# Half sums of two passes joined by accumulating transfers, rotation of quarter columns, and index scores in PSUM, in a hybrid decode step

## The chip, the cores and the metric

One core of one Trainium2 chip. The metric is device time in microseconds of one execution of the whole program. The engines named are TensorE (PE; its weight loads PEld), VectorE (DVE), ScalarE (ACT), GpSimd (POOL) and SyncE (SP, which only issues transfers here).

## What is computed

One layer of a hybrid decoder step over 1024 prompt tokens and 64 sample tokens (together TOK = 1088) with a model width of 2048. In float32 throughout:

```python
h = rmsnorm(x, g) * (1 + scale) + shift            # scale, shift, gate from silu(c) @ w_ada + b_ada
q_a,k_a,v_a,z_a,q_b,k_b,v_b,z_b,q_i,k_i,w_i,g_a,g_b = split(h @ w_in)
# q_a, k_a, q_b, k_b and the indexer's q_i, k_i are rotated by position
# branch A: dilated windows (128,1), (512,4), (2048,16), merged by their softmax denominators
# branch B: I[t,s] = sum_h w_i[t,h] * relu(q_i[t,h] . k_i[s]); top 256 keys of each query, attention over those
y = x + gate * ((sigmoid(g_a) * ((o_a*silu(z_a)) @ w_pa) + sigmoid(g_b) * ((o_b*silu(z_b)) @ w_pb)) @ w_out)
y = rmsnorm(y, g_final)                            # keys and values are outputs too
```

`h @ w_in` is the largest part: 76 column tiles of 128 besides the three of the indexer.

## The kernel before, in words

Everything lies transposed: a column of the projection is a tile of 128 partitions by 1088 tokens. Each factor of a product is split into a high and a low part (`h_hi`, `h_lo`, `wc_hi`, `wc_lo`), and three matmuls make one full product.

**Start (to about 150 us).** Rows are normed, transposed and modulated; the adaLN weights are streamed; products for the first two indexer tiles run among them. SP saves the upper half of `h` into the scratch `merged`.

**Index (about 150 to 264 us).** `third_products` makes the third indexer tile. `leave_index` rotates the tiles out of PSUM into `qi_t` and `ki_two` through `rot_a` and `rot_b`. Then for each of seven query tiles (`PICKS`, widths 384 to 1088) and four heads PE makes scores, ACT writes their relu into `relu_s` (SBUF, two buffers), and DVE multiplies by `wi_tok` and sums into `acc` (`index_scores`), which SP stores in the scratch `score`. POOL meanwhile makes the activation sums S1 to S4 of the scheme below, once `ki_two` is stored.

**Two passes of steps.** The projection is done by pairs of columns with a seven-product scheme over quarters (two halves of tokens, FIRST and SECOND, and even and odd tiles of the inner dimension). The inner dimension is halved too: steps 0 to 37 (`PAIRS` = 38) make all column pairs over the first half, steps 38 to 75 over the second. A step is products P1, P4 of the step before, P2, P6, P5, P7, P3. Their results leave the banks as quarters "11", "12", "22", "21" of a `col` tile (two buffers): copies by ACT (`act_out_of`) and additions by DVE (`add_bank`). P6, P7 and P3, P4 accumulate onto banks that must have been read out before (`p1_out`, `u2_out`, `p5_out`, `c22_out`, `c21_out`). Each engine's order is written out by hand in `pe`'s `step`, `act_step`, `dve_step`, `pool_step`, `sp_step`. The weights of the next step are summed on POOL (`weight_sums`, line 2548 is the first of its four), and split by ACT (`high_weights`), DVE (`low_weights_dve`) and POOL (`low_weights`).

In the first pass SP stores each half sum in the scratch `proj`. In the second SP loads it back into `col` ahead of the step (`load_part`). DVE adds "11", "12", "22" to it from the bank (`direct`), or ACT copies the bank into `snap` and POOL adds that (`add_snap`). The second pass takes first the rotated columns: 2 + 4 (kind "class") + 2 + 4 + 1 pairs, then 3 plain pairs, then 22 whose columns get SiLU or sigmoid ("curved", `act_ended`). Rotation is done in the step: DVE multiplies the swapped halves by sine (`swapped`), POOL the column by cosine (`by_cosine`), DVE adds (`turned`); class columns go out regrouped through `turn_o`.

**Picks.** The top 256 of each query tile are found by 32 rounds on DVE (`pick_round`, lines 2301 and 2303: the eight largest, then strike them out of `work`), spread over the steps through `rounds`. SP loads `work` and stores the mask. Picks 0 to 3 lie in steps 2 to 36 with four rounds a step and one step without rounds between picks, picks 4 to 6 in steps 53 to 73 with four or five and none between.

**After the passes (from about 2060 us)** come attention of both branches and the merge with the output projection.

## Time and profile before

| | us |
|---|---|
| median of three runs | 3195.18 (3194.44 to 3195.89) |
| the profiled execution | 3194.12 |
| its span, first to last instruction | 3192.6 |
| busy in it: PE, DVE, POOL, ACT | 2918.5, 2176.8, 1171.8, 1030.2 |

A profile is one execution. "Busy" is time in which an engine worked on an instruction; the granted clock is TensorE's, 1.00 being 2.4 GHz. A wait names who ended it. Line numbers are those of the kernel before.

### The profile page before, as it was taken

What the parts mean: (1) busy time and instruction counts of PE and PEld (TensorE: products, weight loads), DVE (VectorE), ACT (ScalarE), POOL (GpSimd) and SP (SyncE); (2) the same over time, 40 slices, a digit from 0 to 9 for tenths busy, and PEclk for the clock granted to TensorE, in tenths of its full rate; (3) what the DMA queues carried; (4) which work ended last, traced back from release to release, by engine and by line L of the source; (5) the groups of instructions that cost most, each with busy time, mean ns of one, the idle gap of its engine ahead of it and who ended that gap; (6) DMA issues with size and microseconds to landing.
All of it is one profiled execution on the core that took longest, in us unless ns stands there. A gap on an engine that the chain in (4) does not pass through costs nothing. (4 is left out here: it accounts for less than half of the span.)

```text
span 3192.6 us, 56880 instructions
## 1 busy us (share of the span) xinstructions
PE 2918.5 (91%) x21635; PEld 2728.3 (85%) x21635; DVE 2176.8 (68%) x2948; ACT 1030.2 (32%) x1748; POOL 1171.8 (37%) x1096
## 2 busy tenths in 40 slices
PE   5858999999999888889988988989999999999998
PEld 4736999999999888889987888978877897998987
DVE  4496876877767698997887878556654553654655
ACT  5214333223232321112332323266433332333333
POOL 3162666643333365565554545433224101000000
PEclk8979999999999999999999999999999999999999
DMA  9923455444454543434443434466259775584673
GB/s 348 366 65 105 143 165 178 157 156 150 134 162 128 202 139 119 133 133 149 143 134 126 138 130 134 154 216 192 87 157 293 236 249 182 179 274 130 206 238 99
DMA packets 415737, 544.88 MB, mean 171 GB/s; under 512 B 29572, under 2 KB 327236, under 8 KB 412484
## 3 DMA queue, kind: packets, MB, share of 16 engines
q1 hardware_dynamic: 401478, 498.50, 49.1%
q0 software_dynamic: 12944, 42.23, 4.1%
q8 instruction: 83, 1.36, 0.2%
q10 hardware_dynamic: 1152, 2.13, 0.2%
q14 instruction: 80, 0.66, 0.1%
HBM read 407.84 MB, written 137.04 MB: 171 GB/s over the span
## 5 line engine op out<-in xcount | busy, mean ns | idle before, releaser
L3118 PE MATMUL banks<-h_hi,wc_lo 128*128 128x272 f32 x4256 | 1242.0, 292 | 0.0
L3116 PE MATMUL banks<-h_hi 128*128 128x272 f32 x2432 | 720.3, 296 | 107.5 <-DVE col L2880 58.4
L3118 PEld LDWEIGHTS banks<-h_hi,wc_lo 128*128 128x128 f32 x4256 | 816.2, 192 | 0.0
L3117 PE MATMUL banks<-h_lo,h_hi 128*128 128x272 f32 x2432 | 714.8, 294 | 0.0
L3116 PEld LDWEIGHTS banks<-h_hi 128*128 128x128 f32 x2432 | 471.8, 194 | 119.5 <-issue 57.4
L3116 PE MATMUL banks<-h_hi,wc_hi 128*128 128x272 f32 x1824 | 530.4, 291 | 23.4 <-ACT col L2700 15.2
L3117 PE MATMUL banks<-h_lo,wc_hi 128*128 128x272 f32 x1824 | 528.1, 290 | 0.0
L3117 PEld LDWEIGHTS banks<-h_lo,h_hi 128*128 128x128 f32 x2432 | 472.5, 194 | 0.0
L3116 PEld LDWEIGHTS banks<-h_hi,wc_hi 128*128 128x128 f32 x1824 | 345.5, 189 | 29.8 <-issue 29.0
L3117 PEld LDWEIGHTS banks<-h_lo,wc_hi 128*128 128x128 f32 x1824 | 345.8, 190 | 0.0
L2029 DVE TENSOR_TENSOR u_lo<-u_raw,u_hi 128x1536 fp32r<-128x1536 f32 (+1 forms) x96 | 195.8, 2039 | 202.8 <-ACT u_hi L1943 202.4
L2880 DVE TENSOR_TENSOR col<-banks,col 128x544 f32<-128x544 f32 x309 | 220.8, 720 | 135.4 <-PE banks L3118 126.2
L2301 DVE MAX8 best<-work 128x8 f32<-128x1088 f32 x224 | 287.7, 1284 | 19.3 <-DMA work<-scratch_score 17.9
L1943 ACT CAST u_hi<-u_raw 128x1536 fp32r<-128x1536 f32 (+1 forms) x96 | 162.8, 1696 | 414.0 <-PE banks L2287 232.0
L2680 ACT CAST h_hi<-xn_t 128x512 fp32r<-128x512 f32 x304 | 188.8, 622 | 305.5 <-PE banks L3118 183.9
L2303 DVE MATCH_REPLACE8 work<-best,work 128x1088 f32<-128x1088 f32 x224 | 285.9, 1276 | 0.6 <-issue 0.6
L2854 DVE TENSOR_TENSOR wc_lo<-raw,wc_hi 128x512 fp32r<-128x512 f32 x152 | 158.0, 1040 | 164.0 <-ACT wc_hi L2680 163.6
L2680 ACT CAST wc_hi<-raw 128x512 fp32r<-128x512 f32 x228 | 141.2, 620 | 343.0 <-PE banks L3118 343.0
L2854 DVE TENSOR_TENSOR wc_lo<-xn_t,h_hi 128x512 fp32r<-128x512 f32 x228 | 225.6, 990 | 32.7 <-ACT h_hi L2680 24.1
L2576 POOL TENSOR_TENSOR wc_lo<-raw,wc_hi 128x512 fp32r<-128x512 f32 x76 | 101.0, 1329 | 360.7 <-ACT wc_hi L2680 360.5
L2285 PE MATMUL banks<-u_hi,m_hi 128*128 128x512 f32 x512 | 200.5, 392 | 5.6 <-DVE u_lo L2029 5.6
L2287 PE MATMUL banks<-u_lo,m_hi 128*128 128x512 f32 x512 | 200.2, 391 | 0.0
(340 smaller groups left out, 5374.8 us busy)
## 6 DMA issues: line engine op xcount, KB each, us to landing
scratch_proj<-col SPq DMA_DIRECT2D x144, 544.0 KB, 4.1
raw<-in_w_in SPq DMA_DIRECT2D x76, 1024.0 KB, 5.9
u_raw<-in_w_out SPq DMA_DIRECT2D x96, 512.0 KB, 5.0
col<-scratch_proj SPq DMA_DIRECT2D x76, 544.0 KB, 3.6
ada_w<-in_w_ada SPq DMA_DIRECT2D x16, 2048.0 KB, 14.0
u_raw<-in_w_pb SPq DMA_DIRECT2D x48, 512.0 KB, 4.9
gate_w<-in_w_ada SPq DMA_DIRECT2D x16, 1024.0 KB, 5.9
u_raw<-in_w_pa SPq DMA_DIRECT2D x48, 256.0 KB, 3.2
```

Of the source, the lines that this page charges most:

```text
L1943: nc.scalar.copy(u_hi[u % 2][:, 0:ks, :], u_raw[:, u, 0:ks, :]).then_inc(u_hi_set, 1)
L2029: nc.vector.tensor_tensor(u_lo[u % 2][:, 0:ks, :], u_raw[:, u, 0:ks, :], u_hi[u % 2][:, 0:ks, :], ALU.subtract).then_inc(u_lo_set, 1)
L2285: nc.tensor.matmul(dst, high, hi[:, x, :], start=first, stop=False)
L2287: mm = nc.tensor.matmul(dst, high, lo[:, x, :], start=False, stop=last)
L2301: nc.vector.max(best8[:], work[:])
L2303: nc.vector.match_replace(work[:], best8[:], work[:], TAKEN)
L2680: nc.scalar.copy(wc_hi(c), src).then_inc(wc_hi_set, 1)
L2854: nc.vector.tensor_tensor(wc_lo[c][:], src, wc_hi(c), ALU.subtract).then_inc(lo_dve, 1)
L2880: nc.vector.tensor_tensor(dst, pair_bank(bank), dst, ALU.add).then_inc(out, 1)
L3116: nc.tensor.matmul(dst, hi[:, j, :], high, start=(fresh and j == 0), stop=False, skip_group_check=True)
L3117: nc.tensor.matmul(dst, hi[:, j, :], low, start=False, stop=False, skip_group_check=True)
L3118: mm = nc.tensor.matmul(dst, lo[:, j, :], high, start=False, stop=(j == KB - 1), skip_group_check=True)
```

## The change

Four parts.

1. **Second pass.** A second-pass step now leaves its banks as a first-pass step does. Then `add_halves`, on POOL's queue, joins the two halves of the inner dimension by a transfer that accumulates: into `proj` in DRAM (`proj += col`) for rotated and plain columns, into `col` (`col += proj`) for curved ones, on which ACT then works and which SP stores. `load_part`, `snap` and `add_snap` go.
2. **Rotation.** Rotated columns are read back by quarters of tokens, 104 blocks, four in each of the steps 40 to 52 and 54 to 66: SP loads the quarter, and once more with its halves swapped (`load_rotated`), DVE makes two products and a sum (`rotate`), SP stores. Block b+1 is loaded behind the store of block b. The tables hold half of the tokens at a time. Class columns go into the scratch `merged`.
3. **Index.** Relu writes back into PSUM, and DVE reads PSUM; PE's banks are free after DVE's sum (`acc_step`) instead of after the relu. The third indexer weights and the tables are loaded ahead of the stores of `h`. POOL's sums come before the store of `ki_two`, in two pieces each; the first block is split ahead of the last query tile.
4. **Picks.** Picks 0 to 4 lie in steps 2 to 36, five and four rounds a step, with no step between; picks 5 and 6 in steps 39 to 54 and 56 to 71 with two rounds a step.

The core of the diff:

```diff
-        for x in range(4):
-            for s in range(2 + 9 * x, 10 + 9 * x):
-                PICK_ROUNDS[s] = (x, 4)
-        PICK_LATE = SNAP_STEPS[0] + 1
-        for x in range(3):
+        for x in range(5):
             for y in range(7):
-                PICK_ROUNDS[PICK_LATE + 7 * x + y] = (4 + x, 5 - y % 2)
+                PICK_ROUNDS[2 + 7 * x + y] = (x, 5 - y % 2)
+        for x in range(2):
+            for y in range(16):
+                PICK_ROUNDS[PAIRS + 1 + 17 * x + y] = (5 + x, 2)
...
+        ROT_COLS = [(s, q) for s in TURN_STEPS for q in range(2)]
+        ROT_BLOCKS = [(s, q, 2 * half + y) for half in range(2) for s, q in ROT_COLS for y in range(2)]
+        HALF_BLOCKS = len(ROT_BLOCKS) // 2
+        ROT_AT = {b: PAIRS + 2 + b // 4 + b // HALF_BLOCKS for b in range(len(ROT_BLOCKS))}
...
                     if h == 0:
-                        nc.vector.tensor_scalar(out, relu_s[:, n % 2, 0:width], wi_tok[:, t, h:h + 1], None,
+                        nc.vector.tensor_scalar(out, flat(pick_bank(n), P, width), wi_tok[:, t, h:h + 1], None,
                                                 ALU.mult).then_inc(acc_step, 1)
...
+        def load_rotated(sp, b):
+            (s, q, y), g = ROT_BLOCKS[b], b % 2
+            ts, lo, up = slice(y * PC, (y + 1) * PC), slice(0, HD // 2), slice(HD // 2, HD)
+            src = scr["proj"][T0_OF(s) + q]
+            sp.wait_ge(added[s % 2][q], 16 * added_cols(s))
+            if b >= 2:
+                sp.wait_ge(rot_out[g], rot_outs(b - 2))
+            sp.dma_start(rot_x[:, g, 0, :], src[:, ts]).then_inc(rot_in[g], 16)
+            for to, of in ((lo, up), (up, lo)):
+                sp.dma_start(rot_x[to, g, 1, :], src[of, ts]).then_inc(rot_in[g], 16)
...
+        def rotated_at(sp, s, j):
+            if (s, j) in ROT_IN:
+                b = ROT_IN[s, j]
+                store_rotated(sp, b)
+                if b == HALF_BLOCKS - 1:
+                    load_tables(sp, 1)
+                if b + 1 < len(ROT_BLOCKS):
+                    load_rotated(sp, b + 1)
...
+        def add_halves(pool, s, q):
+            par = s % 2
+            if s == PAIRS:
+                for x in range(2):
+                    pool.wait_ge(col_stored[x][q], 16 * stored_cols(PAIRS, x))
+            for out in ((c11_out, c21_out), (c22_out, c12_out))[q]:
+                pool.wait_ge(out, s + 1)
+            ours, half = col[par][:, q, :], scr["proj"][T0_OF(s) + q]
+            if curved(s):
+                pool.dma_start(ours, half, accum_op=ALU.add).then_inc(added[par][q], 16)
+            else:
+                pool.dma_start(half, ours, accum_op=ALU.add).then_inc(added[par][q], 16)
...
         def pool_step(pool, s):
             low_weights(pool, s, 5)
-            if s and turns(s - 1):
-                by_cosine(pool, s - 1, 2)
-            if snaps(s):
-                add_snap(pool, s, 0)
+            if s > PAIRS:
+                add_halves(pool, s - 1, 1)
             low_weights(pool, s, 6)
-            if s and turns(s - 1):
-                by_cosine(pool, s - 1, 3)
+            if s > PAIRS:
+                add_halves(pool, s - 1, 0)
             if s + 1 < STEPS:
                 weight_sums(pool, s + 1)
...
-                    nc.scalar.activation(relu_s[:, n % 2, 0:width], flat(pick_bank(n), P, width),
+                    nc.scalar.activation(flat(pick_bank(n), P, width), flat(pick_bank(n), P, width),
                                          ACT.Relu, scale=IH ** -0.5 * ID ** -0.5).then_inc(relu_set, 1)
...
+        def rotate(dve, b):
+            (s, _, y), g = ROT_BLOCKS[b], b % 2
+            ts, x, swapped = slice(y % 2 * PC, (y % 2 + 1) * PC), rot_x[:, g, 0, :], rot_x[:, g, 1, :]
+            dve.wait_ge(rot_in[g], 48 * (b // 2 + 1))
+            dve.wait_ge(rot_ready, 80 + 48 * (b // HALF_BLOCKS))
+            nc.vector.tensor_tensor(x, x, rot_cos[:, ts], ALU.mult).then_inc(rot_mul, 1)
+            nc.vector.tensor_tensor(swapped, swapped, rot_sin[:, ts], ALU.mult).then_inc(rot_mul, 1)
+            dve.wait_ge(rot_mul, 2 * b + 2)
+            if not by_class_of(b):
+                nc.vector.tensor_tensor(x, x, swapped, ALU.add).then_inc(rot_add, 1)
+                return
...
         def rounds(dve, s, n):
+            if (s, n) in ROT_IN:
+                rotate(dve, ROT_IN[s, n])
...
-            parts = ((0, 1, 2, 2) if late else (1, 1, 1, 1)) if all_ == 4 else ((0, 1, 2, 2) if late else (1, 1, 1, 2))
+            parts = (0, 1, 0) if all_ == 2 else (0, 1, 2) if late else (1, 1, 1)
```

## Rows read from the trace of the kernel before

**Rows 1.** Windows by stage: busy time and instructions of each engine, PEclk, DMA, GB/s.
```profile
150.00:264.00 114.00, 62.73 (x372) 36.92 (x370) 99.05 (x98) 29.42 (x46) 50.65 (x14) 0.76 0.30 94
264.00:1083.00 819.00, 812.62 (x6814) 807.91 (x6807) 599.51 (x720) 253.09 (x435) 393.12 (x312) 1.00 0.47 149
1083.00:2060.00 977.00, 852.49 (x6404) 838.42 (x6404) 784.37 (x848) 254.61 (x389) 509.21 (x351) 0.95 0.42 138
```

**Rows 2.** Timeline of POOL: start, duration; the first weight sum of a step.
```profile
343.12 1.30 POOL L2548 TENSOR_TENSOR xn_t<-raw 128x512 f32<-128x512 f32 x1 [0.17 <-POOL wc_lo L2576]
...
364.23 1.29 POOL L2548 TENSOR_TENSOR xn_t<-raw 128x512 f32<-128x512 f32 x1 [0.17 <-POOL wc_lo L2576]
...
1083.18 1.30 POOL L2548 TENSOR_TENSOR xn_t<-raw 128x512 f32<-128x512 f32 x1 [0.17 <-POOL wc_lo L2576]
...
1123.46 1.55 POOL L2548 TENSOR_TENSOR xn_t<-raw 128x512 f32<-128x512 f32 x1 [0.17 <-POOL wc_lo L2576]
...
1151.72 1.29 POOL L2548 TENSOR_TENSOR xn_t<-raw 128x512 f32<-128x512 f32 x1
...
1672.96 1.29 POOL L2548 TENSOR_TENSOR xn_t<-raw 128x512 f32<-128x512 f32 x1 [0.17 <-POOL wc_lo L2576]
...
1707.28 1.29 POOL L2548 TENSOR_TENSOR xn_t<-raw 128x512 f32<-128x512 f32 x1 [0.17 <-POOL wc_lo L2576]
...
2037.65 1.29 POOL L2548 TENSOR_TENSOR xn_t<-raw 128x512 f32<-128x512 f32 x1 [0.17 <-POOL wc_lo L2576]
```

**Rows 3.** Waits from 1083 to 2060 us: who, for whom, total, times, longest.
```profile
ACT col L2714 <- DVE col L2880: 242.4, 38, 17.1
POOL col L2571 <- ACT snap L2708: 198.2, 27, 18.4
```

**Rows 4.** DVE instructions on tile col: count, shortest, median, longest in ns.
```profile
L2880 DVE TENSOR_TENSOR col<-banks,col x203: 707/718/728, 1050.1 to 2073.3; 128x544 f32<-128x544 f32 x102
...
L2905 DVE TENSOR_TENSOR col<-col,turn_b x36: 712/1795/1802, 1131.3 to 1460.9; 128x544 f32<-128x544 f32 x36
```

**Rows 5.** DMA issues: count, KB each, median us from issue to landing.
```profile
col<-scratch_proj SPq DMA_DIRECT2D x76, 544.0 KB, 3.6
...
gates<-scratch_proj SPq DMA_DIRECT2D x64, 192.0 KB, 2.4
...
scratch_resid<-prep_lo POOLq DMA_DIRECT2D x8, 544.0 KB, 4.7
```

**Rows 6.** Timeline of SP where it issues transfers back to back: start, duration.
```profile
2070.26 0.38 SPq L737 DMA_DIRECT2D k_t<-scratch_proj  x1
2070.68 0.51 SPq L737 DMA_DIRECT2D v_t<-scratch_proj  x1
```

**Rows 7.** Timeline of DVE in two first-pass steps and at one change of pick.
```profile
598.24 1.28 DVE L2301 MAX8 best<-work 128x8 f32<-128x1088 f32 x1
...
601.02 1.50 DVE L2854 TENSOR_TENSOR wc_lo<-xn_t,h_hi 128x512 fp32r<-128x512 f32 x1
...
613.07 1.29 DVE L2854 TENSOR_TENSOR wc_lo<-raw,wc_hi 128x512 fp32r<-128x512 f32 x1 [2.01 <-ACT wc_hi L2680]
...
617.94 0.73 DVE L2880 TENSOR_TENSOR col<-banks,col 128x544 f32<-128x544 f32 x1 [0.95 <-PE banks L3118]
...
1683.76 1.29 DVE L2301 MAX8 best<-work 128x8 f32<-128x1088 f32 x1 [8.96 <-DMA work<-scratch_score]
```

**Rows 8.** Timeline of DVE in the index stage; in brackets its idle time before.
```profile
156.75 1.29 DVE L364 TENSOR_TENSOR w_lo<-w_raw,w_hi 128x1088 fp32r<-128x1088 f32 x1 [12.91 <-DMA irot_sin<-in_rot]
...
191.39 7.75 DVE L2344 TENSOR_SCALAR acc<-relu_s,wi_tok 128x384 f32<-128x384 f32 x1 [0.60 <-ACT relu_s L2841]
...
199.27 14.99 DVE L2347 SCALAR_TENSOR_TENSOR acc<-relu_s,wi_tok,acc 128x384 f32<-128x384 f32 x3
```

**Rows 9.** Timeline of PE: the third products, and P1 of the first step.
```profile
158.09 0.59 PE L392 MATMUL banks<-h_hi,w_hi 128*68 128x384 f32 x1 [7.50 <-DVE w_lo L364]
...
264.05 0.39 PE L3116 MATMUL banks<-h_hi,wc_hi 128*128 128x272 f32 x1
```

More of the change, by code:

```diff
@@ L456, in decode_step @@
         turns = lambda s: kind_of(s) in ("turned", "class")
-        direct = lambda s: turns(s) or s > 0 and turns(s - 1)
-        snaps = lambda s: s >= PAIRS and not direct(s)
         curved = lambda s: s >= PAIRS and not isinstance(kind_of(s), str)
@@ L2336, in index_scores @@
                     low_weights_dve(dve, 0, 1)
+                    low_block(dve, 0)
                 if width < TOK:
@@ L2865, in add_bank @@
         def add_bank(dve, s, x, bank, place, out):
-            q = int(x[1]) - 1
             dve.wait_ge(p_done, done(s, place))
-            if s >= PAIRS:
-                dve.wait_ge(part_landed[s % 2][q], 16 * sum(y % 2 == s % 2 for y in range(PAIRS, s + 1)))
-            if x != "21" and out not in (p1_out, u2_out, p5_out):
-                n = ("11", "12", "22").index(x)
-                if snaps(s):
-                    dve.wait_ge(snap_added, 3 * before(s, snaps) + n + 1)
-                else:
-                    dve.wait_ge((p1_out, u2_out, p5_out)[n], s + 1)
@@ L2877, in add_bank @@
[L2877 to L2878 removed]
+            copied = {"11": p1_out, "12": u2_out, "22": p5_out, "21": e_out}[x]
+            dve.wait_ge(copied, 1 if x == "21" else s + 1)
             dst = of_col(s % 2, x)
             nc.vector.tensor_tensor(dst, pair_bank(bank), dst, ALU.add).then_inc(out, 1)
[L2882 to L2895 removed]
@@ L2931, in dve_step @@
         def dve_step(dve, s):
-            par, more, rot = s % 2, s + 1 < STEPS, turns(s)
-            was = s and turns(s - 1)
+            par, more = s % 2, s + 1 < STEPS
             if s:
@@ L2937, in dve_step @@
                 low_block(dve, 7)
-            if was:
-                turned(dve, s - 1, 1)
-                swapped(dve, s - 1, 2)
-            if direct(s):
-                add_bank(dve, s, "11", BANK_A(par), "P1", p1_out)
             if more:
@@ L2945, in dve_step @@
             rounds(dve, s, 0)
-            if was:
-                turned(dve, s - 1, 2)
-            if s > PAIRS:
-                add_bank(dve, s - 1, "21", BANK_A(1 - par), "P4", c21_out)
-            if was:
-                swapped(dve, s - 1, 3)
             if s == PAIRS:
@@ L2954, in dve_step @@
             add_bank(dve, s, "11", BANK_B, "P2", c11_out)
-            if was:
-                turned(dve, s - 1, 3)
-            if rot:
-                swapped(dve, s, 0)
             if more:
@@ L3140, in step @@
             need(pe, x_lo_set, x_waits[1])
-            need(pe, relu_set, scores)
+            need(pe, acc_step, scores)
             need(pe, c11_out, s)
@@ L3296, in _ @@
                 for h0 in range(0, IH, 2):
-                    need(pe, relu_set, n - 2)
+                    need(pe, acc_step, n - 2)
                     for a in range(0, width, 512):
@@ L3308, in _ @@
             for h in range(IH):
-                need(pe, relu_set, n - (h > 0))
+                need(pe, acc_step, n - (h > 0))
                 half = slice(ID * (h % 2), ID * (h % 2) + ID)
@@ L3320, in _ @@
                 n += 1
-            pe.wait_ge(relu_set, n - 1)
+            pe.wait_ge(acc_step, n - 1)
             step(pe, 0, 0, x_waits=(0, 0, 1, 2, 3, 4, 0), scores=n)
```

344 lines of the change are left out of this document (144 added, 200 removed).

## The prediction

> **What bounds the kernel now.** I read the windows by stage first, then the clock of the steps, then the waits inside the slow stretch, then single instructions.
>
> [Rows 1] cut the span into stages. Up to 150 us the transfers set the pace and the change hardly touches it; after 2060 us comes attention and merging, which it touches only at the seam. From 264 to 1083 us (first pass of the 38 column pairs) TensorE is busy 812.6 of 819 us at full clock: nothing to win there, only to lose. Two stretches are not PE-bound. From 150 to 264 us (index scores) PE is busy 62.7 of 114 us, the granted clock is 0.76 and DVE is busy 99 us. From 1083 to 2060 us (second pass, the same products) PE has 852 of 977 us.
>
> The clock of the steps is the first weight sum of each step on POOL [rows 2]. In the first pass two of them lie 364.23-343.12 = 21.11 us apart, which is the seven products. In the second pass the 37 intervals from 1083.18 to 2037.65 take 954.5 us. The first of them is 40.3 us (transformed activations are reloaded), the second 28.3, and the other 35 average (2037.65-1151.72)/35 = 25.3 us. With 21.11 in 36 of the 37 the stretch would last 40.3+36x21.11 = 800 us, so 154 us are there to be had, and no more.
>
> Why the second pass is slow stands in [rows 3]: ACT waits 242 us for DVE's additions to `col`, POOL waits 198 us for the copies into `snap`, which it then adds. A result leaves its bank by ACT, POOL and DVE in a chain, or, in the rotating steps, by DVE alone, and the bank is needed again. There is also a wait for `work` at each change of pick.
>
> **Second pass: what goes.** Gone are the loads of the half sums into `col` (76 of 544 KB), `snap`, POOL's additions, the direct additions and the in-line rotation with `by_cosine`. A step then leaves its banks exactly as in the first pass: four ACT copies and three DVE additions of 0.72 us [rows 4]. Nothing of that part is a reason for more than 21.11 us, because the first pass does it with the weights' work at 21.11. What is new must fit beside it.
>
> **Second pass: what comes.** (a) Two accumulating transfers of 544 KB a step from POOL, either into DRAM or into `col`. No row shows one. Nearest is a plain POOL transfer of 544 KB at 4.7 us to landing [rows 5]; the accumulating one reads its target too, so I take 5 to 10 us and, because POOL must write its descriptors, under 1 us of POOL each. Behind the waiting POOL stand `low_weights` 6 and the sums of the next step; ACT and PE need these 12 us or more into the step, and POOL was busy 393 of 819 us in the first pass, 10 of 21 us a step [rows 1]. The column buffer is wanted again when the copy of "11" two steps on must be ready for P6. With the second transfer issued about 8 us into the next step, that gives some 20 us. I put it at 0; it costs nothing below zero either, since the banks do not wait for it. If one took over 10.5 us of service, two would fill a step and set it. (b) Curved columns: activation and store move later behind the transfer; ACT has (819-253)/819 of the first-pass time idle [rows 1]. 0. (c) The rotation: 13 turned or class pairs x 2 columns x 4 quarters = 104 blocks, four in each of 26 steps (PAIRS+2 to PAIRS+14, PAIRS+16 to PAIRS+28).
>
> This last is where I see the new limit, so in detail. Block b+1 is loaded by SP only behind the store of block b, which waits for b's rotation, and DVE waits in order for its landing, with its bank additions and weight splits queued behind. So rotate, store issue, three load issues, landing, rotate is one chain, although there are two buffers. Issues on SP take 0.38 to 0.51 us each [rows 6]: the last load goes out about 1.4 us after the rotation. Its landing: 2.4 us for 192 KB, 3.6 us for 544 KB [rows 5], and these loads total 272 KB; 2.6 taken. That gives 4.0 us, with bounds 3.3 (0.37 apart, 2.2 to land) and 5.1 (0.5 apart, 3.6). The rotation is three additions or products of 128x272 with both inputs in SBUF. 544 elements take 0.71 us [rows 4], so 272 take 0.36 by length; with a fixed part for each instruction I take 0.43, three 1.3 us. Where POOL works at the same time such an instruction stretches (0.712 least, 1.795 median for 544 [rows 4]), so 1.9 us is taken, bounds 1.4 and 2.3.
>
> Between rotations DVE has other work, which hides part of the 4.0 us: after the first an addition and a split (1.7), after the second a pick round and a split (2.8+0.9 = 3.7; a round is 601.02-598.24 = 2.78 us [rows 7]), after the third an addition and two splits (2.6), after the fourth a round, an addition and a split (4.4). A step therefore takes 4.0+4.0+4.0+4.4 and four rotations of 1.9 = 24.0 us. Lower bound: 3.3+3.7+3.3+4.4 and 4x1.4 = 20.3, under PE's 21.11, so 21.11. Upper bound: 5.1x4 and 4x2.3 = 29.6 us. DVE may run about 4 us late before P4 waits for its "22", once in each of the two groups of 13: 8 us back. The stretch: 40.3 + 22 (second interval, no rotation in it) + 9x21.11 + 26x24.0 - 8 = 868 us, against 954.5: **-86 us** (bounds -153 and about +60).
>
> The Trainium skill, "DMA: Bandwidth & Descriptors", section "Rules for kernel authors", says of two transfers to disjoint partition halves: "Don't bother", they serialize; it speaks against loading the swapped half rows by two transfers. Its fit in "Anatomy of one DMA" is 2.0 us plus bytes over 436e3 per us; by it the last 68 KB land in 2.2 us, a step is 22.9 us, and the kernel 29 us faster than my sum. No row shows a 68 KB load alone.
>
> **First pass.** It now holds five picks instead of four, at five and four rounds a step. In a step with four rounds DVE was idle 2.01+0.95 us [rows 7]; one more round of 2.78 just fits, and four-round steps between catch up. But at the four changes of pick there is no longer a step without rounds: `work` must be stored and the next score loaded while DVE stands. At such a change in the second pass DVE waited 8.96 us [rows 7] and the interval came to 1707.28-1672.96 = 34.3 us [rows 2], 9 over the average. In the first pass c21 is copied by ACT and only "22" is due, 3 us into the next step; DVE stands 5 to 6 us and loses about 3. Four times: **+12 us** (bounds 0 and 40). The second pass loses its two such changes; that is inside its 86.
>
> **Index scores.** Three things. The third weight tile and tables are issued before the stores of h: today DVE stands 12.91 us for a table [rows 8], and PE 7.50 us for DVE's split before the third products [rows 9]. That is 7.5 us. Then the long one: DVE's reads of `relu_s` and `acc` (both SBUF) run beside POOL's block sums, and a product over 384 elements takes 7.75 us, the next three 5.0 each [rows 8]; an instruction with one input in PSUM never stretches (0.707 to 0.728 us over 203 [rows 4]). With the scores in PSUM DVE needs 4 heads x 5312 columns x 1.32 ns = 28 us, plus 5 for memsets and tails, 6 for tails that still meet POOL (now in halves), 4 for the pipeline of matmul, relu and sum, which now waits for the sum to free the bank, and 3.7 for splits and block 0, moved ahead. Some 46.7 us in all, from 191.4 [rows 8] less 7.5: P1 begins near 230.5 instead of 264.05 [rows 9]. POOL's sums no longer wait for `ki_two`, so they start and end earlier still and are not late for P6. PE waits for `acc_step`, not `relu_set`, behind which its next pair of heads stands; that is in the 4. **-34 us** (bounds -42 and -15). The stall of step 0 stays.
>
> Of the behaviour behind it, the Trainium skill, "SBUF — State Buffer", section "Who interferes with whom", has a rule that speaks against the rotation here: a DVE instruction with two SBUF inputs and a POOL instruction that reads SBUF block each other for the whole instruction. By it each of a block's three could wait for a POOL sum of 1.3 us, 5.2 us a block, 37 us a step and the kernel some 340 us above my sum, if they always met; that is the far end of rival C below; [rows 4] show that the median does stretch, the least doesn't, and POOL is idle half of a step.
>
> **Seam.** `q_class` is read from another scratch with the same pattern, last activations go behind three turned tiles: 0, within 3 us.
>
> **Sum**, against the profiled execution's own 3194.1 us (span 3192.6 and 1.5 around it; the median of the runs is 3195.2): 3194.1-86+12-34 = **3086 us**.
>
> **Rivals.** (A) The rotation's chain hides: landing near 2.2 us and little meeting with POOL, steps of 21.1 to 22. Then 3194-153+12-34 = 3019, with a cheap first pass 3003. For it: the lower bounds of landing and rotation come to 20.3 us together; against: that leaves DVE 0.8 us of slack, and the loads queue behind larger ones. Chance 0.27. (B) The forecast, steps of 22.5 to 26.5, 3045 to 3150: 0.50. (C) Slower: the chain pays for the added transfers. Each of its four landings stands behind 1 MB of weights or an accumulating 544 KB on the same engines. With 26x the step's excess against 34-12+(954.5-252.3+8) the turning point is 732/26 = 28.2 us a step, that is 5.2 us from rotation to landing with 1.9 for the rotation; at 31 us it is 3194+73 = 3267. Accumulating transfers of over 14 us service, which would set every step at 28, belong here. Against: DMA share is 0.42 in the stretch [rows 1]. Chance 0.10. (D) The scores gain only their 7.5 us, because another wait (the bank freed late, PE at half clock) takes the place: 3112; 0.08. The rest, 0.05, lies between B and C.
>
> Range for 8 in 10: 3000 to 3180; it takes in A, B, D and leaves out C and the ends. Chances: a change under 0.2% (6 us, about what a measurement of this kernel can tell from none) 0.03; faster 0.87; slower 0.10.
>
> **What would show it.** Weight sums 21.1 us apart in the last steps and in the plain gap, about 24 in rotating ones, with DVE waiting for `rot_x`'s transfer; if it waits for nothing and steps are 21.1, A is right. No score instruction over 1.5 us and first products near 230. At each change of pick in the first pass one long interval. If intervals are even but long everywhere in the second pass, the accumulating transfers set them, and my zero was wrong.

## The result and the profile after

The changed kernel takes 3154.8 us (median of 4 runs, 3148.5 to 3159.8) against 3195.5 us: a ratio of 0.987, interval 0.985 to 0.989. It is 41 us faster; 108 were forecast. The direction held, and so did the range of 3000 to 3180, the size did not: the median lies just above rival B's 3045 to 3150, in the stretch between B and C that had a chance of 0.05. The profiled execution took 3148.5 us with a span of 3146.9, so 45.7 us less span than before.

The windows by stage; columns as in [rows 1]. The line numbers from here on are those of the kernel that a row is from.

```profile
150.00:225.00 75.00, 59.28 (x337) 34.99 (x339) 65.93 (x98) 27.92 (x45) 50.02 (x23) 0.86 0.47 157
225.00:1030.00 805.00, 784.72 (x6553) 777.43 (x6546) 648.47 (x781) 241.14 (x416) 380.68 (x304) 0.99 0.45 147
1030.00:2020.00 990.00, 897.41 (x6800) 891.26 (x6799) 668.97 (x867) 316.21 (x492) 393.98 (x310) 0.95 0.63 165
```

TensorE is still idle for some 90 us in the second pass, though DVE's busy time there fell (784 of 977 us before, 669 of 990 now). The clock of the steps, the answer to [rows 2] and [rows 9]: POOL's first weight sum of a step, and P1 of the first step on PE.

```profile
228.41 0.39 PE L3084 MATMUL banks<-h_hi,wc_hi 128*128 128x272 f32 x1
...
582.87 1.30 POOL L2571 TENSOR_TENSOR xn_t<-raw 128x512 f32<-128x512 f32 x1 [0.17 <-POOL wc_lo L2595]
612.22 1.53 POOL L2571 TENSOR_TENSOR xn_t<-raw 128x512 f32<-128x512 f32 x1 [0.17 <-POOL wc_lo L2595]
...
1066.89 1.30 POOL L2571 TENSOR_TENSOR xn_t<-raw 128x512 f32<-128x512 f32 x1 [0.17 <-POOL wc_lo L2595]
...
1116.35 1.56 POOL L2571 TENSOR_TENSOR xn_t<-raw 128x512 f32<-128x512 f32 x1
...
1137.45 1.55 POOL L2571 TENSOR_TENSOR xn_t<-raw 128x512 f32<-128x512 f32 x1
...
1475.97 1.89 POOL L2571 TENSOR_TENSOR xn_t<-raw 128x512 f32<-128x512 f32 x1
1493.36 1.57 POOL L2571 TENSOR_TENSOR xn_t<-raw 128x512 f32<-128x512 f32 x1
...
1838.80 1.90 POOL L2571 TENSOR_TENSOR xn_t<-raw 128x512 f32<-128x512 f32 x1
...
1984.21 1.56 POOL L2571 TENSOR_TENSOR xn_t<-raw 128x512 f32<-128x512 f32 x1
```

Cut at the same events, before and after stand so (the last row is the span less the start of the last weight sum):

| stretch | before | after | difference | forecast |
|---|---|---|---|---|
| up to P1 of the first step | 264.05 | 228.41 | -35.6 | -34 |
| P1 to the first sum of the second pass | 819.1 | 838.5 | +19.4 | +12 |
| second pass, 37 intervals | 954.5 | 917.3 | -37.2 | -86 |
| behind the last weight sum | 1155.0 | 1162.7 | +7.7 | 0 |

In the second pass the first two intervals take 49.5 us. The first group of 13 rotating steps takes 1475.97-1137.45 = 338.5 us, 26.0 a step; the second 345.4, 26.6 a step, with four of 30.8, 28.4, 28.5 and 28.4 us in it. The interval behind a group is 17.4 and 18.7 us, and every other 21.1.

What waits from 1060 to 2000 us, the answer to [rows 3] (total, times, longest):

```profile
DVE rot_x L2889 <- DMA rot_x<-scratch_proj: 169.0, 82, 4.9
POOL col L2588 <- DVE col L2881: 157.4, 15, 16.1
POOL scratch_proj L2590 <- DVE col L2881: 152.7, 14, 13.2
...
ACT col L2722 <- DMA scratch_proj<-col: 118.4, 12, 13.6
...
PE banks L3084 <- DVE col L2881: 83.3, 24, 7.2
```

DVE waits for the landing of the blocks to rotate. DVE's bank additions are queued behind the rotation, and both TensorE, which needs the bank, and POOL's accumulating transfers wait for them. One rotating step, on DVE, POOL and SP in turn (it is one of the shortest; most of those with four plain blocks take 25.3 to 27.3 us):

```profile
1372.82 2.12 DVE L2893 TENSOR_TENSOR rot_x<-rot_x 128x272 f32<-128x272 f32 x1
...
1380.25 0.44 DVE L2889 TENSOR_TENSOR rot_x<-rot_x,rot_cos 128x272 f32<-128x272 f32 x1 [3.61 <-DMA rot_x<-scratch_proj]
...
1385.29 0.44 DVE L2889 TENSOR_TENSOR rot_x<-rot_x,rot_cos 128x272 f32<-128x272 f32 x1 [0.32 <-DMA rot_x<-scratch_proj]
...
1390.21 0.44 DVE L2889 TENSOR_TENSOR rot_x<-rot_x,rot_cos 128x272 f32<-128x272 f32 x1 [1.81 <-DMA rot_x<-scratch_proj]
...
1395.50 0.43 DVE L2889 TENSOR_TENSOR rot_x<-rot_x,rot_cos 128x272 f32<-128x272 f32 x1
1395.85 2.17 DVE L2890 TENSOR_TENSOR rot_x<-rot_x,rot_sin 128x272 f32<-128x272 f32 x1
1398.06 2.11 DVE L2893 TENSOR_TENSOR rot_x<-rot_x 128x272 f32<-128x272 f32 x1
...
1372.12 1.19 POOL L2590 DMA_DIRECT2D scratch_proj<-col  x1
...
1375.42 0.43 SPq L2401 DMA_DIRECT2D rot_x<-scratch_proj  x1
1375.88 1.35 SPq L2403 DMA_DIRECT2D rot_x<-scratch_proj  x2
```

From the end of one rotation to the start of the next it is 5.3 us (1374.94 to 1380.25), then 3.8, 3.7 and 4.0; these are called the gaps. The rotations take 1.3 us three times and 4.7 once (1395.50 to 1400.17), when POOL works too. Together 25.2 us, and the step is 25.2 us: the chain of rotations closes on itself, with nothing else in it. Over all steps the first gap has a median of 5.5 us (4.3 to 6.2), the other three 3.8, 3.8 and 4.0.

### The profile page after: what moved, and what is told of

Same layout as the page of the kernel before. It is cut to its first block and busy times, and to the rows that moved or that the text cites. A ratio compares the mean times of both kernels' runs of the same rounds, so it can differ in the third digit from the quotient of the medians.

```text
span 3146.9 us, 57322 instructions
## 1 busy us (share of the span) xinstructions
PE 2920.1 (93%) x21635; PEld 2736.4 (87%) x21635; DVE 2076.1 (66%) x3024; ACT 1079.2 (34%) x1830; POOL 1042.6 (33%) x1057
## 3 DMA queue, kind: packets, MB, share of 16 engines
q8 instruction: 83, 1.36, 0.2%
## 5 line engine op out<-in xcount | busy, mean ns | idle before, releaser
L2722 ACT COPY col<-banks 128x544 f32<-128x544 f32 x304 | 186.2, 612 | 727.1 <-PE banks L3086 604.1
L3084 PEld LDWEIGHTS banks<-h_hi,wc_hi 128*128 128x128 f32 x1824 | 347.3, 190 | 21.8 <-issue 18.5
L2311 DVE MAX8 best<-work 128x8 f32<-128x1088 f32 x224 | 287.8, 1285 | 21.3 <-DMA work<-scratch_score 19.4
L2881 DVE TENSOR_TENSOR col<-banks,col 128x544 f32<-128x544 f32 x229 | 164.9, 721 | 145.4 <-PE banks L3086 136.4
L2864 DVE TENSOR_TENSOR wc_lo<-xn_t,h_hi 128x512 fp32r<-128x512 f32 x228 | 197.2, 865 | 33.8 <-ACT h_hi L2699 25.2
L2296 PE MATMUL banks<-u_hi,m_lo 128*128 128x512 f32 x512 | 200.3, 391 | 0.0
```

What stands on the lines that cost most here:

```text
L2296: nc.tensor.matmul(dst, low, hi[:, x, :], start=False, stop=False)
L2311: nc.vector.max(best8[:], work[:])
L2722: nc.scalar.copy(of_col(par, x), pair_bank(bank)).then_inc(out, 1)
L2864: nc.vector.tensor_tensor(wc_lo[c][:], src, wc_hi(c), ALU.subtract).then_inc(lo_dve, 1)
L2881: nc.vector.tensor_tensor(dst, pair_bank(bank), dst, ALU.add).then_inc(out, 1)
L3084: nc.tensor.matmul(dst, hi[:, j, :], high, start=(fresh and j == 0), stop=False, skip_group_check=True)
```

## The experiments

The theory (T): the loads of the rotated blocks and the rotations form one chain on DVE and SP, which sets the rotating steps. The rivals: the accumulating transfers themselves set them (R1); DVE's work and its meeting with POOL set them, whatever the loads do (R2); the late stores of curved columns set them (R3). All edits are made to the changed kernel.

Early loads, their placed version, the sum into another tile, the stores from ACT and the last kernel ran four or five times; each of the others ran once. The changed kernel itself wasn't run again beside them; the kernel before was, and took 3191.1, 3195.2 and 3192.7 us in the median of the three sets. Three kernels whose edits leave the second pass alone (changes of pick, scores in SBUF, seam) have it at 924.4, 919.2 and 924.1 us in their traces, against 917.3. So a few us between totals, and under 10 us in the second pass of single traces, tell nothing.

**The rotation left out.** No block is loaded, rotated or stored, so queries and keys stay unrotated. All the rest, the accumulating transfers too, stays.

```diff
-            if (s, j) in ROT_IN:
+            if (s, j) in ():
...
-            if (s, n) in ROT_IN:
-                rotate(dve, ROT_IN[s, n])
```

> Leaves the rotation of the 26 projected columns out altogether (their quarters are neither loaded, nor rotated, nor stored; the output differs in all that uses them). If the rotation with its loads is what stretches the steps from 21.1 to 26.3 us, then all intervals of the second pass after the first two fall to 21.1 us and the stretch from first to last weight sum falls from 917 us to about 49+35x21.1 = 790 us, the whole by about 127 us to some 3020. If the accumulating transfers or ACT's chain have a share, intervals stay above 21.1, most of all in the curved steps.

3020.0 us. The first and the last weight sum of the second pass:

```profile
1061.44 1.30 POOL L2567 TENSOR_TENSOR xn_t<-raw 128x512 f32<-128x512 f32 x1 [0.17 <-POOL wc_lo L2591]
...
1850.78 1.56 POOL L2567 TENSOR_TENSOR xn_t<-raw 128x512 f32<-128x512 f32 x1
```

That is 789.3 us, and all intervals behind the first two are 21.1. So the rotation costs 128 of the 917 us, and behind the first two intervals the accumulating transfers, activations and stores by themselves cost nothing. R1 and R3 are out as causes that act alone.

**Loads two blocks ahead.** Block b+2 is asked for behind the store of block b, into the buffer that this store frees.

```diff
-                if b + 1 < len(ROT_BLOCKS):
-                    load_rotated(sp, b + 1)
+                if b + 2 < len(ROT_BLOCKS):
+                    load_rotated(sp, b + 2)
...
             if s == PAIRS + 1:
                 load_rotated(sp, 0)
+                load_rotated(sp, 1)
```

> One change to the changed kernel: block b+2 instead of b+1 is loaded behind the store of block b, so each load has a whole further block of time. Theory (landing is exposed four times a step): DVE's waits for rot_x, 169 us in all, go nearly to nothing and rotating steps fall from 26.3 to what DVE's own work allows, about 22 to 23.5 us: 70 to 100 us faster than the changed kernel. Rival (the steps are long because the rotation meets POOL and because DVE is full): the steps stay at 25 or more, the waits only move.

3120.7 us (3115.8 to 3126.4), ratio to before 0.977 [0.976, 0.979], 34 us under the changed kernel, where at least 70 were expected. DVE's waits for `rot_x` fell from 169.0 us to this:

```profile
DVE rot_x L2890 <- DMA rot_x<-scratch_proj: 34.3, 34, 3.5
```

Steps are 24.4 and 25.9 us in the two groups (26.0 and 26.6 before the edit). Much less waiting and only a little less time: something took over. (What, the next run's rows show; here SP stands 325 us in front of its loads, waiting for stores.)

**And rotations away from POOL's sums.** In addition each of a step's four rotations moves one place later, so that none stands at the step's start and two stand behind its last splits; a pick round goes to the start. SP's order stays.

```diff
-            if (s, n) in ROT_IN:
-                rotate(dve, ROT_IN[s, n])
+            if (s, n) in ROT_IN and n:
+                rotate(dve, ROT_IN[s, n - 1])
...
+            if (s, n) in ROT_IN and n == 3:
+                rotate(dve, ROT_IN[s, 3])
```

> The prefetch of e2_prefetch, and DVE's order changed: no rotation at the start of a step, where POOL begins its splits and sums; the pick round stands there, and the four rotations come after the second, third and (two) last weight splits. In the changed kernel the rotation at the start takes 4.7 us, the three others 1.3 us. Theory (meeting POOL costs 3.4 us a step): rotations of 1.3 to 2.5 us, steps at 21.1 to 22 us and 20 to 40 us faster than e2_prefetch. Rival: POOL's sums meet other instructions instead, nothing gained over e2_prefetch.

3120.0 us (3108.3 to 3123.7), ratio 0.976 [0.974, 0.979]: no gain over the early loads alone. But the groups parted: 22.9 us a step in the first, 27.5 in the second, where the later steps alternate between 26 and 30. SP's own waits point to the reason (1060 to 1900 us; line 2400 is the wait in front of a load for the store out of the same buffer):

```profile
SPq L2400 <- DMA scratch_proj<-rot_x: 149.9, 69, 5.9
...
SPq L2400 <- DMA scratch_merged<-turn_o: 63.3, 24, 4.9
```

With the load directly behind the store that frees its buffer, SP stands 240 us (with 26.4 in a third such row) until its own stores have landed, and curved columns and weights queue behind it. The early loads had put a new wait where the old one was; the next run tests that.

**The same, with the sum written to another tile.** The last of the three instructions writes into `turn_o`, as it does for class blocks anyway. The load then needs only the rotation, not the store's landing. In exchange DVE waits, before it writes into `turn_o`, for the landing of the store of the block before.

```diff
-                sp.wait_ge(rot_out[g], rot_outs(b - 2))
+                sp.wait_ge(rot_add, b - 1)
...
-                nc.vector.tensor_tensor(x, x, swapped, ALU.add).then_inc(rot_add, 1)
...
+                dve.wait_ge(rot_out[(b - 1) % 2], rot_outs(b - 1))
...
+                nc.vector.tensor_tensor(turn_o[:, 0:PC], x, swapped, ALU.add).then_inc(rot_add, 1)
```

> The version with early loads and with rotations moved away from POOL's sums, and in it the last of a block's three instructions writes into turn_o instead of the block's own buffer, so that SP can issue the load two blocks ahead without waiting for the landing of the store before it. If SP's standing behind its own stores (57 us in the second group of that version) delays the curved columns and so the banks, steps of the second group fall from 28 to 23-25 us and the kernel from 3120 to about 3080. If the second group is long because three activations and two stores of a curved column are themselves too much for the step, nothing changes: 3115 to 3125.

3046.4 us (3045.1 to 3049.0), ratio 0.954 [0.953, 0.956]; 74 us from this one edit, where about 40 were expected. The second pass:

```profile
1062.27 1.30 POOL L2572 TENSOR_TENSOR xn_t<-raw 128x512 f32<-128x512 f32 x1 [0.17 <-POOL wc_lo L2596]
...
1877.25 1.56 POOL L2572 TENSOR_TENSOR xn_t<-raw 128x512 f32<-128x512 f32 x1
```

That is 815.0 us, 26 above the version without any rotation; the groups run at 22.1 and 22.5 us a step. SP's waits for a store in front of a load are gone, and DVE's for `rot_x` are 0.8 us in one place; for stores out of `turn_o` it waits 36 us in all, in 29 places, and TensorE's wait for DVE's bank additions fell from 83.3 to 7.2 us. Of the 128 us that the rotation costs in the changed kernel, 102 were the order of its loads, stores and rotations, not its work.

**The two halves of the rotation apart.** First all its transfers, with DVE working on 2 of a block's 272 columns (the last addition of class blocks stays whole). Then all of DVE's work and the stores, with only the first two blocks loaded; later blocks rotate what stands in the buffers, once the store of two blocks before has landed.

```diff
-            nc.vector.tensor_tensor(x, x, rot_cos[:, ts], ALU.mult).then_inc(rot_mul, 1)
+            nc.vector.tensor_tensor(x[:, 0:2], x[:, 0:2], rot_cos[:, 0:2], ALU.mult).then_inc(rot_mul, 1)
```

> The rotation's transfers all stay, but DVE works on 2 of the 272 columns of a block (the class blocks' last addition stays whole), so what is computed is not rotated. By the theory of the chain, a step is 4 gaps of about 4 us from rotation to landing plus four short rotations, under TensorE's 21.1: steps of 21.1 to 22 and about 3020 to 3040 in all. By the rival, in which the loads and their waits alone make the slow steps, steps stay at 24 or more and the kernel over 3090.

```diff
-                if b + 1 < len(ROT_BLOCKS):
+                if b + 1 < 2:
                     load_rotated(sp, b + 1)
...
-            dve.wait_ge(rot_in[g], 48 * (b // 2 + 1))
+            dve.wait_ge(rot_in[g], 48)
+            if b >= 2:
+                dve.wait_ge(rot_out[g], rot_outs(b - 2))
```

> Only the first two blocks are loaded; the later ones rotate what stands in the buffers, with DVE's three instructions and the stores unchanged, so what is computed is wrong for all later blocks. If DVE's work and its meeting with POOL's sums cost by themselves, steps are as with early loads, 24 to 24.5 us, and the kernel about 3100. If they cost only because they stand in one chain with the landings, steps are 21.1 to 22 and the kernel 3020 to 3045.

Transfers alone: 3104.4 us, steps 23.9 and 24.7. DVE's work alone: 3047.4 us, steps 22.5 and 22.4. The first came out as its rival said (steps of 24, over 3090), not as the theory did (21.1 to 22). The second came near the theory (21.1 to 22, up to 3045). DVE's work costs 1.3 us a step by itself and not 3: R2 is small. But the transfers alone still cost 3 us a step, though by my sum of gaps they fit under 21.1. The second pass of DVE's work alone, 819.1 us, is as long as that with early loads and sums into `turn_o`, 815.0: there the loads cost nothing beyond DVE's work. The timeline of DVE with the transfers alone shows the missing part, with POOL's second accumulating transfer and SP's loads beside it:

```profile
1377.35 2.00 DVE L2893 TENSOR_TENSOR rot_x<-rot_x 128x2 f32<-128x2 f32 x1
...
1379.91 2.12 DVE L2864 TENSOR_TENSOR wc_lo<-raw,wc_hi 128x512 fp32r<-128x512 f32 x1
1387.61 0.16 DVE L2889 TENSOR_TENSOR rot_x<-rot_x,rot_cos 128x2 f32<-128x2 f32 x1 [5.58 <-DMA rot_x<-scratch_proj]
...
1378.98 1.18 POOL L2590 DMA_DIRECT2D scratch_proj<-col  x1
...
1380.31 1.20 SPq L2403 DMA_DIRECT2D rot_x<-scratch_proj  x2
```

The load's last issue ends at 1381.5 and DVE goes on at 1387.6, 6.1 us later, where such loads land in 2.4 us in the median. The accumulating transfer was issued just before. The gaps are 8.3, 3.8, 3.8 and 4.5 us, the four short rotations 3.3: 23.7, again the whole step. (Over all steps the first gap has a median of 8.3 us, 4.7 to 9.3.) What a shorter rotation gave back, the first landing took.

**Plain transfers in place of accumulating ones.** The second half overwrites instead of being added, so the sums of the two passes are missing.

```diff
-pool.dma_start(half, ours, accum_op=ALU.add)
+pool.dma_start(half, ours)
```

> The transfers on POOL's queue copy instead of accumulating (one half of the inner dimension is lost, the output differs). Theory: they are off the path, so intervals in the second pass stay within 0.3 us (26 rotating, 21.1 at the end). Rival: reading the target too loads the engines, so that landings of rot_x get shorter and rotating steps 1 us or more shorter. POOL's transfer should land 2 to 3 us sooner than 7.

3110.0 us, steps 24.1 and 25.2, so 1.9 and 1.4 us shorter, where the theory had expected 0.3 at most; the rival's 1 us or more came true. The transfers' rows, of the changed kernel and then of this one (KB each, median us to landing):

```profile
col<-scratch_proj POOLq DMA_DIRECT2D x44, 544.0 KB, 6.9
scratch_proj<-col POOLq DMA_DIRECT2D x32, 544.0 KB, 7.0
```
```profile
col<-scratch_proj POOLq DMA_DIRECT2D x44, 544.0 KB, 5.2
scratch_proj<-col POOLq DMA_DIRECT2D x32, 544.0 KB, 5.1
```

And the first gap behind the step's start in this kernel (first line the end of the rotation, 1360.30):

```profile
1358.51 1.79 DVE L2893 TENSOR_TENSOR rot_x<-rot_x 128x272 f32<-128x272 f32 x1
...
1364.24 0.46 DVE L2889 TENSOR_TENSOR rot_x<-rot_x,rot_cos 128x272 f32<-128x272 f32 x1 [2.24 <-DMA rot_x<-scratch_proj]
```

3.9 us instead of 5.3 (medians over all steps 4.1 and 5.5). The first rotation fell too, from 4.7 to 4.1 us, as POOL's part of it got shorter (an issue of 0.57 us instead of 0.88 to 1.2, sums of 1.3 instead of 1.9). So R1 has a share after all, through the chain: a small load behind an accumulating transfer of 7 us comes late, and that costs nothing where no load is there (the first run).

**Curved stores from ACT.** The two stores are issued by ACT behind its own activations, so that they can't stand behind a rotation on SP.

```diff
-                if s and (s <= PAIRS or curved(s - 1)):
+                if s and s <= PAIRS:
                     store_col(sp, s - 1, q)
...
+            if ended:
+                store_col(act, s - 1, 1)
...
+            if ended:
+                store_col(act, s - 1, 0)
```

> One change to the changed kernel: the finished curved columns are stored from ACT's queue, right behind ACT's work on them, instead of from SP's, where the store stands behind waits for rotated blocks. In the changed kernel ACT waits 118 us for these stores (12 times) and the rotating steps beside curved ones take 26.6 us on average, four of them 28.4 to 30.8; SP's late stores also stand ahead of the loads of keys at the end. Theory: that wait goes, the four long steps fall to 26 or 27, the loads at the seam come 8 us earlier: 15 to 25 us faster in all. Rival (the wait only covers the rotation's pace): steps unchanged, only the seam's 8 us.

3151.9 us (3144.4 to 3154.4), ratio 0.986 [0.984, 0.988]: no gain that can be told from none, where 15 to 25 us were expected. ACT's wait for these stores has left the top of the list, and its wait for PE has risen from 268.4 to:

```profile
ACT col L2722 <- PE banks L3090: 384.9, 127, 11.1
```

The 118 us were slack, not cost: a second witness against R3.

**The changes of pick.** Rounds of a pick go 4, 5, 5, 5, 5, 5, 3 over its seven steps, and in the first step they stand late.

```diff
-                PICK_ROUNDS[2 + 7 * x + y] = (x, 5 - y % 2)
+                PICK_ROUNDS[2 + 7 * x + y] = (x, (4, 5, 5, 5, 5, 5, 3)[y])
...
-            parts = (0, 1, 0) if all_ == 2 else (0, 1, 2) if late else (1, 1, 1)
-            if late and n == 1:
+            parts = (0, 1, 0) if all_ == 2 else (0, 0, 2) if late else (1, 1, 1)
+            if late and n == (1 if all_ == 2 else 2):
```

> One change to the changed kernel: in the first pass a pick begins only in the third of the four places of its first step and its last step has three rounds (4,5,5,5,5,5,3 instead of 5,4,5,4,5,4,5), so that storing one mask and loading the next scores has some 6 us more. Theory: the three long intervals (29.35, 27.24, 28.74 us against 21.11 and 22.44) are DVE's wait for that load; they fall to within 1.5 us of the others, and the kernel gets 14 to 19 us faster. Rival: the five-round steps alone fill DVE, then extra time appears in other intervals.

3143.6 us. The first pass, between its first weight sum and that of the second pass, goes from 821.5 to 804.8 us. In the changed kernel three changes of pick are the only steps clearly over their neighbours, by 8.2 (the pair 582.87 and 612.22 above), 4.8 and 6.3 us; here these are 2.2, 0.6 and 0.8. The total of this one run is only 11 us lower, with the second pass of its trace 7 us longer. At the first of them, in the changed kernel, DVE stood so long:

```profile
594.41 1.29 DVE L2311 MAX8 best<-work 128x8 f32<-128x1088 f32 x1 [9.69 <-DMA work<-scratch_score]
```

**Index scores back in SBUF.** ACT's output goes to `relu_s` again; order and placement of the rest stay as changed.

```diff
-                        nc.vector.scalar_tensor_tensor(out=out, in0=flat(pick_bank(n), P, width),
+                        nc.vector.scalar_tensor_tensor(out=out, in0=relu_s[:, n % 2, 0:width],
...
-                    nc.scalar.activation(flat(pick_bank(n), P, width), flat(pick_bank(n), P, width),
+                    need(act, acc_step, n - 1)
+                    nc.scalar.activation(relu_s[:, n % 2, 0:width], flat(pick_bank(n), P, width),
```

> One change to the changed kernel: relu writes to SBUF again and DVE reads both inputs there; everything else of the change stays. Theory (with two inputs in SBUF DVE's sums stand still beside POOL's block sums, and that was most of the gain of the index stage): instructions over 384 elements of 2.4 us and more while POOL works (its pieces are now half as long), and the first product of the first step 10 to 25 us later than in the changed kernel. Rival (the earlier load, and the earlier POOL sums brought the gain): under 5 us later.

3170.9 us; P1 of the first step stands at 246.89 instead of 228.41, 18.5 us later. DVE on `acc` in the changed kernel, then in this one (shortest, median and longest in ns):

```profile
L2358 DVE SCALAR_TENSOR_TENSOR acc<-banks,wi_tok,acc x21: 617/1017/1354, 185.3 to 229.6; 128x384 f32<-128x384 f32 x3, 128x512 f32<-128x512 f32 x3, 128x640 f32<-128x640 f32 x3, 128x768 f32<-128x768 f32 x3
```
```profile
L2359 DVE SCALAR_TENSOR_TENSOR acc<-relu_s,wi_tok,acc x21: 1017/1351/2922, 187.1 to 248.1; 128x384 f32<-128x384 f32 x3, 128x512 f32<-128x512 f32 x3, 128x640 f32<-128x640 f32 x3, 128x768 f32<-128x768 f32 x3
```

The longest instruction, over 1088 columns, takes 1.35 us in both; with SBUF inputs shorter ones take up to 2.9 us.

**The seam.** The last two column stores of the plain order are issued behind the loads of keys and values.

```diff
+            for q in (1, 0):
+                store_col(sp, LAST - 1, q)
...
-                if s and (s <= PAIRS or curved(s - 1)):
+                if s and s < LAST and (s <= PAIRS or curved(s - 1)):
                     store_col(sp, s - 1, q)
```

> One change to the changed kernel: in the last step SP issues the loads of keys and values before the stores of the curved columns of the step before, for whose activation it otherwise waits. Theory (8 us lost between the last weight sums and 2057 us are SP standing there): PE's wait for kiT of 15.3 us falls to under 8 and the stretch behind the last weight sum is 6 to 9 us shorter than 1162.7 us. Rival: the accumulating transfers and stores on the same engines hold the loads up: under 3 us.

3143.0 us. From the last weight sum to the end it is 1155.2 us instead of 1162.7, which is the time of before, 1155.0. The nine other traces that keep the plain order of these stores have 1161.9 to 1169.0 us there (the last kernel below, with the edit, 1159.8), so the gain is clear and its size is known to some us only. In the changed kernel SP stands at a store until ACT's activation is done, and first behind it come the keys; TensorE pays (SP, then PE):

```profile
2012.94 3.35 SPq L2383 DMA_DIRECT2D scratch_proj<-col  x2
2016.55 0.39 SPq L741 DMA_DIRECT2D k_t<-scratch_proj  x1
...
2035.57 1.09 PE L1101 MATMUL banks<-ident,k_t 128*128 128x128 f32 x4 [15.28 <-DMA kiT<-scratch_proj]
```

With the edit that row of PE shows 1.19 us idle:

```profile
2023.60 0.63 PE L1103 MATMUL banks<-ident,k_t 128*128 128x128 f32 x4 [1.19 <-DMA kiT<-scratch_proj]
```

**All of it.** Early loads, placement, sums into `turn_o`, shifted rounds and the late stores, each as above.

> All parts together: early loads, rotations placed, sums into turn_o, rounds of the first pass shifted so that its changes of pick have slack, and the last two plain-order column stores issued behind the loads of keys and values. First pass about 16 us shorter than after (measured alone: 821.5 to 804.8), seam 7 us shorter (measured alone: 1162.7 to 1155.2), second pass as in the kernel of the run beside it: if the parts add, 23 us under that run, that is about 3055 to 3095.

3029.0 us (3022.0 to 3031.4, 5 runs), ratio to before 0.948 [0.947, 0.949], 126 us under the changed kernel and 164 under the one before (3192.7 beside these runs). The second pass in this kernel:

```profile
1030.00:1900.00 870.00, 844.66 (x6652) 839.76 (x6652) 655.58 (x846) 306.75 (x482) 398.58 (x309) 1.00 0.73 188
```

Its granted clock is 1.00, the full 2.4 GHz, where the changed kernel, with the same work and TensorE idle for some 90 us between, has a mean of 0.95. It is 17.4 us under the run with sums into `turn_o` beside it, where 23 were expected, with 7.5 from the first pass and 7.4 from the seam; the total lies under the 3055 to 3095 expected, as that run had already come out lower. The shifted rounds gave 17 alone and only 7.5 here; one change of pick, of 29.1 us, was left, and why was not tried.

## Why the prediction was right, and where it failed

**What bounds the kernel, and the chain: right.** In the rotating steps DVE waits for `rot_x`, the plain steps are 21.1 us apart, and the steps close as rotations and gaps. Rival A's time, 3019, is what the kernel without the rotation takes, 3020.0; that they agree to 1 us is luck, since its second pass is 12 us shorter than A's (789.3 against 801) and the stretch behind it some 13 longer (1167.6 against 1155). A's 3003 with a cheap first pass is a slip: 3194-153-34 is 3007.

**The size of a rotating step: the term that failed.** 24.0 us was forecast, and 26.0 and 26.6 were measured: the sum left out what happens where the first load of a step meets the accumulating transfer. Term by term in the step shown above, with four plain blocks (measured terms rounded):

| term | forecast | measured |
|---|---|---|
| gap behind the first rotation | 4.0 | 5.3 |
| the second, third and fourth gaps | 4.0, 4.0, 4.4 | 3.8, 3.7, 4.0 |
| the four rotations | 4 x 1.9 = 7.6 | 3 x 1.27 + 4.7 = 8.5 |
| step | 24.0 | 25.2 |

Issue and landing without such a transfer in front were sized well (3.7 to 4.0 us), and what they fell short by, the rotations exceeded; that these two cancel is luck. The first gap was not sized well: the chain and the accumulating transfer were each costed alone, the transfer at 0 because no bank waits for it, and their meeting wasn't costed. With its median of 5.5 us over all steps it is 1.5 us a step over the forecast, some 40 of the 60 us by which the 26 steps exceed 26 times 24.0. It recurs, since the second transfer goes out at the start of each step, while the first rotation runs and just ahead of the load behind it (1372.12 and 1375.42 above). The plain transfers showed that 1.4 us of it are due to the accumulation; with them the first group ran at 24.1 us a step, the forecast's size. And the rotation's 1.9 us was a mean of two states, where one of four meets POOL and the other three hardly ever do. The Trainium skill, "SBUF — State Buffer", section "Who interferes with whom", has the two block each other for the whole instruction; the trace agrees for that one (2.1 to 2.2 us against 0.43), and the far end of 37 us a step that it gave was nowhere near.

The rest of the 2.3 us lies mostly in steps of class blocks, which I costed like others. Their last addition takes 0.63 us in the median instead of 0.44, and in the second group every second one has a further addition (0.21 us) and a further store (0.51 us on SP, ahead of the next load), beside the curved stores. Each of these is in the chain, and the four such steps take 28.4 to 30.8 us. With the chain cut they fell to between 23 and 25. That it is these parts is argued from the rows; no run takes them out. The 30.8 has something more: it is the step behind the last change of pick, and the load of its first block, issued behind the saved mask and the next scores, makes DVE wait 4.93 us in a gap of 7.4 instead of 4.0, which wasn't isolated either. In sum: 684 us for the 26 steps, less 6 behind the groups, against 616: 62 us too many. The first two intervals gave 13 back (49.5 for 62.3), as I left the reload at the length it had before. Together this is the 49 us between 868 and 917.

**Accumulating transfers: 6.9 us in the forecast's 5 to 10, and 0 was wrong only through the chain.** Their issue takes 0.88 to 1.2 us of POOL, a little more than the 1 us allowed.

**First pass: the mechanism right, the size not.** 19.4 us instead of 12. I took 3 us for each of four changes from the idle DVE of 5 to 6 us; three of them showed, at 8.2, 4.8 and 6.3, with DVE idle up to 9.69, close to the 8.96 of [rows 7] that I had argued down.

**Index scores: right in total, and in where P1 stands** (228.4, forecast 230.5), with no product of the scores over 1.36 us. But the split was off: 18.5 us come from PSUM, and 17.2 of the 35.6 remain with the scores in SBUF. I had 7.5 for the tables and the rest for PSUM; the rest, about 10 us, comes even to scores in SBUF, because they meet less of POOL's sums. The timeline of that kernel has the first four products in 10.8 us, which took 22.7 in [rows 8]:

```profile
184.36 2.64 DVE L2356 TENSOR_SCALAR acc<-relu_s,wi_tok 128x384 f32<-128x384 f32 x1 [1.04 <-ACT relu_s L2855]
187.12 8.12 DVE L2359 SCALAR_TENSOR_TENSOR acc<-relu_s,wi_tok,acc 128x384 f32<-128x384 f32 x3
```

That this is POOL's doing is argued from the order of its sums; no run isolates it.

**Seam: wrong.** 0 within 3 us was forecast, and 7.7 was measured and removed by moving two issues. I had named the queue that the activations are moved past on ACT, but not what stands behind SP's wait for them.

**A fallen theory of my own.** After the forecast I took the late curved stores for a cost, and the early loads for the cure. The one gave nothing; the other gave a third to a half of what it promised, until SP's wait for its own store was seen. Not tried: one transfer in place of the two for the swapped halves, so what that would give isn't known.

## What to carry to other kernels

A prefetch is only as early as the wait in front of its issue: if the load's buffer is freed by a store's landing, the queue stands for that landing, and everything in it does. Writing the result to a third place gave 74 us here, although DVE then waited 36 us for stores out of that place. When a wait shrinks and the time hardly does, read the waits of the issuing queue next. And a term costed at zero because nobody waits for it must be weighed against the small transfers that are released at about the same moment.

## What the runs showed of the hardware

An accumulating transfer of 544 KB from POOL's queue lands in 6.9 to 7.0 us, a plain one of the same shape in 5.1 to 5.2; POOL spends 0.88 us on issuing the one and 0.57 on the other. A block's load of 272 KB in three transfers, which takes 3.7 to 4.0 us from rotation to rotation, takes 5.5 in the median behind an accumulating transfer (in the step shown its first issue comes 3.3 us behind that transfer's), 4.1 behind a plain one, and 8.3 where it comes sooner behind the accumulating one (0.9 us in the step shown). The 68 KB loads themselves land in 2.4 us in the median. The fit of the Trainium skill, "DMA: Bandwidth & Descriptors", section "Anatomy of one DMA", stated there for transfers from GpSimd, would give 2.2 for these from SP, and that difference isn't what the forecast missed by.

An addition of only 128x2 elements with both inputs in SBUF, 0.16 us in the median, took 2.00 us beside POOL's work (1377.35 above): what it pays there is a wait, not a slower rate.
